# Four tiles of x ahead of set-up, per-row waits in the output gate, and the second block of g loaded from two queues

## The reference

```python
for layer in range(2):
    h = rmsnorm(x, norm_w[layer])
    if layer % 2 == 0:
        u, g_a, q, k, v, g_b = split_cols(h @ ev_w_in, ...)
        a_out = s5_mixer(u, ...) * silu(g_a)     # g = gelu(y); g * sigmoid(g @ w_glu + b_glu)
        b_out = swa_mixer(q, k, v, ...) * silu(g_b)
        mix = concatenate([a_out, b_out]) @ ev_w_out
    else:
        q, k, v, r, a_lr = split_cols(h @ od_w_in, ...)
        mix = gla_mixer(q, k, v, a_lr, ...) * silu(r) @ od_w_out
    x = x + mix
return rmsnorm(x, final_norm)
```

## Time and profile before

| | us |
|---|---|
| median of three runs (1696.63 to 1697.51) | 1696.81 |
| the profiled execution | 1697.39 |
| its span in the profile | 1695.6 |
| TensorE busy | 1642.8 (97%) |
| VectorE busy | 822.4 (49%) |
| ScalarE busy | 631.0 (37%) |
| GpSimd busy | 277.8 (16%) |

### The profile page before, as it was taken

How to read it: one execution, slowest core, us unless ns; L and a number is a source line. 1 busy time by engine, 2 the same in 40 slices (tenths; PEclk the granted TensorE clock), 3 DMA queues, 4 the chain that set the end, 5 groups by cost and what they waited for, 6 DMA issues and landing times.

```text
span 1695.6 us, 22567 instructions
## 1 busy us (share of the span) xinstructions
PE 1642.8 (97%) x7898; PEld 1332.0 (79%) x7898; DVE 822.4 (49%) x1655; ACT 631.0 (37%) x1584; POOL 277.8 (16%) x500
## 2 busy tenths in 40 slices
PE   6999999999999799999999999999999999999997
PEld 4777788777777578888778888888888888878886
DVE  6744545667666473543552334333334443254443
ACT  6522334666666472332461222222222232131121
POOL 3883000000000431200000122212221221000000
PEclk9999999999999899999999999999999999999999
DMA  5466544454444946222242333333323332276663
GB/s 215 145 180 187 152 152 134 143 167 140 139 149 127 276 108 240 100 82 93 78 155 98 114 109 115 113 103 109 128 96 101 128 103 81 94 240 190 191 189 109
DMA packets 222216, 236.18 MB, mean 139 GB/s; under 512 B 53112, under 2 KB 169496, under 8 KB 222104
## 3 DMA queue, kind: packets, MB, share of 16 engines
q1 hardware_dynamic: 221528, 233.59, 43.5%
q10 hardware_dynamic: 576, 1.15, 0.2%
HBM read 140.12 MB, written 94.57 MB: 138 GB/s over the span
## 4 chain that ended last, share of the span: by engine, by line
PE 61%; DVE 2%; ACT 1%; DMA 1%; issue 0%; SPq 0%; POOLq 0%; POOL 0%; DVEq 0%; ACTq 0%
PE odd_bank L2143 29%; PE odd_bank L2298 10%; PE odd_bank L2189 10%; PE odd_bank L2168 2%; PE odd_bank L2248 2%; PE odd_bank L2245 2%; PE odd_bank L2246 2%; PE odd_bank L2227 1%; PE odd_bank L2152 1%; PE odd_bank L2203 1%; DMA scr_heads<-odd_ga_min 1%; PE odd_bank L2229 0%; PE odd_bank L2256 0%; PE odd_bank L2230 0%; PE odd_bank L2255 0%
## 5 line engine op out<-in xcount | busy, mean ns | idle before, releaser
L2143 PE MATMUL odd_bank<-ht_hi,odd_w_hi 128*128 128x512 f32 x768 | 318.4, 415 | 0.0
L2143 PE MATMUL odd_bank<-ht_lo,odd_w_hi 128*128 128x512 f32 x768 | 300.6, 391 | 0.0
L2143 PE MATMUL odd_bank<-ht_hi,odd_w_lo 128*128 128x512 f32 x768 | 298.8, 389 | 0.0
L1214 PE MATMUL ev_acc<-ht_hi,ev_w_hi 128*128 128x512 f32 x576 | 239.6, 416 | 2.3 <-DVE ht_lo L926 2.3
L1214 PE MATMUL ev_acc<-ht_hi,ev_w_lo 128*128 128x512 f32 x576 | 226.6, 393 | 0.0
L1214 PE MATMUL ev_acc<-ht_lo,ev_w_hi 128*128 128x512 f32 x576 | 226.3, 393 | 0.0
L1919 DVE COPY odd_stage<-odd_bank 128x512 f32<-128x512 f32 x96 | 66.3, 691 | 224.7 <-PE odd_bank L2143 224.7
L2143 PEld LDWEIGHTS odd_bank<-ht_lo,odd_w_hi 128*128 128x128 f32 x768 | 144.1, 188 | 31.8
L2143 PEld LDWEIGHTS odd_bank<-ht_hi,odd_w_hi 128*128 128x128 f32 x768 | 144.4, 188 | 29.9 <-issue 3.0
L2143 PEld LDWEIGHTS odd_bank<-ht_hi,odd_w_lo 128*128 128x128 f32 x768 | 144.6, 188 | 27.7
L1214 PEld LDWEIGHTS ev_acc<-ht_hi,ev_w_hi 128*128 128x128 f32 x576 | 108.7, 189 | 30.8 <-issue 5.5
(11 more groups left out here) (284 smaller groups left out, 2877.2 us busy)
## 6 DMA issues: line engine op xcount, KB each, us to landing
odd_gl_in<-scr_heads SPq DMA_DIRECT2D x32, 640.0 KB, 4.3
scr_heads<-odd_stage SPq DMA_DIRECT2D x64, 256.0 KB, 2.2
odd_w_raw<-od_w_in SPq DMA_DIRECT2D x24, 512.0 KB, 3.9
ev_w_raw<-ev_w_in SPq DMA_DIRECT2D x17, 512.0 KB, 6.5
ev_s_cos_sin<-scr_s_cos_sin SPq DMA_DIRECT2D x32, 256.0 KB
odd_xo_sum<-x SPq DMA_DIRECT2D x16, 512.0 KB, 4.1
scr_x<-odd_xo_sum SPq DMA_DIRECT2D x16, 512.0 KB, 2.9
scr_gla_mix<-odd_gl_out SPq DMA_DIRECT2D x32, 256.0 KB, 2.1
```

Of the source, the lines that this page charges most:

```text
L1214: mm = pe.matmul(acc[n % 3][:], w[j][:, k, :], h[:, k, t], start=(k == 0 and r == 0), stop=(k == KT - 1 and r == 2))
L2143: mm = pe.matmul(acc[n % 4][:], w[j][:, k, :], h[:, k, t], start=(k == 0 and q == 0), stop=(k == KT - 1 and q == 2))
```

## The change

In the first block, four things at the start: the set-up pieces of VectorE begin only at turn 3 (normed(4) comes there too, then split(1), piece 1, normed(5) and piece 2), so that tiles 0 to 3 run without them, and piece k from 3 on comes two tiles later than before; ScalarE's `exp_decay` stands behind upper(4) and `sines` behind upper(5), with `load_bc` behind it; GpSimd's steps begin at tile 6; and TensorE turns four tiles before slot 0 and tile 4 behind it. In the gate TensorE waits for the low part of each row tile of g just before its products. Of the four loads of the second block of g two stay on SP, and ScalarE issues two behind its last instruction.

```diff
-                def load_g(b):
+                def load_g(b, rows):
...
-                    for k in range(4):
+                    for k in rows:
...
-                        load_g(0)
+                        load_g(0, range(4))
...
-                        load_g(1)
+                        load_g(1, range(2))
...
                     inverse(t)
-                    if t >= 5:
+                    if t >= 6:
                         next(rest, None)
...
-                    if t == 2:
+                    if t == 4:
                         exp_decay()
                     if t == 3:
                         split(1)
-                    if t == 4:
+                    if t == 5:
                         sines()
-                    if t == 5:
                         load_bc()
...
+                for k in range(2):
+                    act.wait_ge(g_st[k], 16 * (NGRP // 2))
+                act.wait_ge(acc_full, 72)
+                for k in range(2, 4):
+                    act.dma_start(in_steps(glu.g_raw[1][1][:, k % 2]), g_steps[k * P:(k + 1) * P, :, GLU_C:2 * GLU_C]
+                                  ).then_inc(glu.g_in[1], 16)
...
                 normed(1)
-                next(rest)
                 for t in range(NT):
                     lower(t)
                     if t == 3:
+                        normed(4)
                         split(1)
-                    if t + 2 < NT:
+                        next(rest)
+                    if t != 2 and t + 2 < NT:
                         normed(t + 2)
-                    if t >= 1:
+                    if t >= 3:
                         next(rest, None)
...
-                for t in range(5):
+                for t in range(4):
                     turn_x(t)
...
+                    if p == 0:
+                        turn_x(4)
                     if p + 5 < NT:
                         turn_x(p + 5)
...
-                    if q == 0:
-                        pe.wait_ge(g_lo_done, 4 * b + 2)
                     if i == 0:
+                        pe.wait_ge(g_lo_done, 2)
                         pe.wait_ge(wg_lo_done, 1)
...
                     for k in range(4):
+                        if b and q == 0:
+                            pe.wait_ge(g_lo_done, 4 * b + k - 1)
```

## The result

The changed kernel's median is 1700.47 us (19 executions, 1698.07 to 1703.39) against 1697.17 (19, 1695.31 to 1699.23) of the kernel before: ratio 1.0021, 95% interval [1.0014, 1.0027]. That is 3.3 us slower by the medians and 3.6 by the ratio. The forecast was 1699.7. The profiled executions differ less, 1698.79 (span 1697.0) against 1697.39 (1695.6): that one is at the low end of its kernel's spread.

A forecast was written before the change was run, and what follows sets the result against it. TensorE's own stream was taken as the bound, VectorE next at the start. Start +6.3, gate -3.8 and border +0.4 gave +2.9: 1700.3 from the profiled 1697.39, or 1699.7 us by the median; range 1692.0 to 1702.5.

The forecast's parts named there:

- the start's +6.3: First block's start: slot 12, waiting for lower(15), starts at 81.2 instead of 74.84, 6.3 us late.
- Start, what comes forward: Start of the first block: first products issue at 22.95 instead of 26.67, 3.7 us earlier.
- Start, the sines ahead of square(7): ScalarE's sines wait for piece 3's angles, square(7) starts at 38.7, turn_x(7) at 42.2; TensorE idles 4.7 us.
- turn_x(7) before 40: Sign at the start: the forecast, with turn_x(7) near 42.2, is wrong if it comes before 40.
- The clock: Behind the 4.7 us hole before turn_x(7): the clock falls to its low level, costing 2.4 us, bounds 0 and 3.6.
- VectorE's chain: Start: VectorE needs 27.0 us from normed(10) at 54.2 to the end of lower(15) at 81.2.
- Gate: Output gate: waits by row remove both TensorE waits for the low part of g, -3.8 us.
- the same kind: Gate's fourth block of columns: its wait is like the third's and goes too, within the -3.8 us.
- Border: Between the blocks: fewer SP loads start the next earlier, ScalarE's loads delay the last store; middle taken, +0.4 us.
- the tiles keep up: Rival at the start: sines cost the tiles nothing, the 2.8 us advance is kept, 1690.6 us; chance 0.17.
- The clock holds: Rival at the start: the clock stays high in the 4.7 us hole, start +3.9, 1697.3 us; chance 0.2.

The follow-up runs named there:

- start_only: The kernel before with the change at the start alone (later set-up, later sines, four tiles ahead of slot 0): 1703.19 us against 1697.20.
- pieces_behind: The whole change, with VectorE's set-up pieces from 7 on run behind lower(15) instead of between the tiles: 1714.78 us against 1696.77 of the kernel before.
- four_tiles: The kernel before with only TensorE's order changed, four tiles ahead of slot 0 and tile 4 behind it: 1703.82 us against 1697.44.
- g1_next_block: The kernel before with row waits, w_out's first low part one accumulation later, and the second g's four loads issued in the next block: 1695.23 us against 1697.44.
- early_setup: The kernel before with four tiles ahead, set-up and sines early, row waits, and w_out's first low part one accumulation later: 1691.28 us against 1697.44.
- gate_only: The kernel before with the gate's waits by row tile alone: 1693.48 us against 1697.20.

## Why the prediction was right, and which steps were off

Forecast +2.9, measured +3.3 (by the ratio +3.6, from 2.4 to 4.6); its three terms, +6.3, -3.8 and +0.4, measured +6.0, -3.7, and +0.1 to +1.0. The mechanisms named for the start and the gate are what the runs show. The steps inside are less good than their sums, and that the start's +6.3 met +6.0 so closely is in part luck: in the two profiles turn_x(7) came 2.0 to 3.1 us earlier than forecast and slot 12 2.7 to 3.9 earlier, and what fills the difference (a profile of before that was itself late, falls of the clock elsewhere, an open rest) is in none of its steps.

- **Start, what comes forward:** products at 22.95 forecast, 21.57 and 22.50 seen. Right: counted from the first transposes it is 13.85 against 13.10 and 13.78, and the 13.10 is of a profile whose fourth tile was turned at the high clock (its first four transposes 0.66 us and not 1.1).
- **Start, the sines ahead of square(7):** the mechanism was right, the size too large. Piece 3 ended at 33.78, not 35.6, and the table load I put behind the wait ran ahead of it (1.3 us). So square(7) came at 35.56 (38.7), turn_x(7) at 39.05 (42.2), the hole was 3.10 (4.7). The prediction had itself named turn_x(7) before 40 as a sign of being wrong, and 39.05 is one (40.16 in start_only): it is the size of this step that failed. The end of upper(4) is also summed 0.2 short (28.2 + 0.96 + 2 x 0.59 is 30.3 and not 30.1), too little to matter here.
- **The clock:** forecast 2.4 behind that hole in every execution. It fell behind that hole (3.09 to 3.10 us) in two of three profiles, the change's and pieces_behind's, for 1.6 each time; in start_only's it stayed there and fell behind slot 8's hole. The size of 2.4 was that of a clock which falls in the hole, and where it did (four_tiles, a hole of 3.54) it cost 2.5. A charge for certain had to be a chance.
- **VectorE's chain:** from normed(10) to the end of lower(15) forecast 27.0, measured 77.27 - 50.23 = 27.0; pieces_behind shows that the pieces set it. Slot 12, forecast at 81.2, was put 3 to 4 too late only because normed(10) was (54.2 against 50.23).
- **What made up for it:** by profiles the start is 4.4 to 4.9 at the block's end (4.9, less the 0.5 by which the first tile came earlier), where the forecast's own steps gave 6.3 at slot 12. By medians it is 6.0, interval 4.8 to 9.0. Some of the difference is falls of the clock that two profiles don't average; the rest is open.
- **Gate:** the form of the wait was worth what was said. But not all of the fourth block's hole goes (0.85 left in the profile, 0 to 2.19 in six profiles with row waits and w_out as before, mean 1.1), because VectorE's first low part of w_out is held by GpSimd ahead of mixed(7), as its durations above show. I had argued this block by "the same kind". Falls of the clock behind the removed holes, which I counted as nothing, can fill the sum (3 of the 10 holes of 1.90 or 1.91 us in the kernels without row waits had one, 1.2 to 1.6 us each): the gate takes 58.3 us in the mean of those six and 61.5 in the mean of the five without row waits.
- **Border:** +0.43 in the two profiles; over all, holes of 11.89 to 14.16, mean 12.9 in six kernels with two queues, and 11.19 to 13.49, mean 12.4 in seven with SP alone. SP is done earlier and the landing of the store then decides, 2.0 us ahead of the block. The rule of the Trainium skill named in the prediction ("DMA: Bandwidth & Descriptors", section "Issuing engines are not separate DMA queues") leans the way these means do. But their difference of 0.5 is no more than their scatter, and in the profile of g1_next_block a store without this traffic lands no sooner (6.8 us).
- **Rivals:** "the tiles keep up" failed where it said (turn_x(7) at 39.05, its limit was 37.5). early_setup shows that most of its 2.8 us are there (2.1 at slot 12 against the mean of the six, 2.3 by medians) if the sines are moved to ScalarE's idle time. "The clock holds" was counted for one hole in every execution, and the clock did hold there in some; the time did not follow, because it fell behind other holes.

## What to carry to other kernels

When side work is moved to start the main stream earlier, count the idle time that it leaves and the bound of the stretch that it enters: with four tiles ahead, the kernel gained some 2 us with the set-up placed early, lost some 6 with the same set-up among the later tiles or where it was before, and waited 17 us for it in a lump behind them. Place it by the idle times of each engine's own timeline (here 4.86 us of ScalarE that nobody used). A wait by rows is worth a whole hole where the rows come one by one (here one of 1.9 us, and part of a second).

## What the runs showed of the hardware

- A small VectorE instruction that starts beside a running GpSimd one can end with it: 1.0 to 1.14 us and not 0.2 (three pairs in pieces_behind). One of 1024 columns that takes 1.22 alone ends 1.07 to 1.09 us after the GpSimd one, and takes 3.37 in gate_only.
- A table load ran before the wait of the activation that it is for: in the change's profile it ended at 32.10, and ScalarE then stood 1.77 us until the angles came (a wait that the program writes ahead of the activation).
- After holes of 1.8 to 3.6 us the granted clock fell to its low level in 10 of 23 cases, in eight of them once work had resumed, for 4 to 8 products. I had expected it to fall during the hole or not at all.
